# Cutting 1056 token columns into 512, 512 and 32 in place of three times 352 in the dense projections of a hybrid decoder step

## The reference, cut to what matters

```python
def mlp(x, w_up, w_down):
    h = jax.nn.relu(x @ w_up)          # 1024 -> 4096
    return (h * h) @ w_down            # 4096 -> 1024

p  = rmsnorm(x, norm_mix) @ w_in_rec                  # 1024 -> 3080, then conv, RG-LRU, gated delta
x += concat(rg_y, dn_y) @ w_out_rec                   # 1024 -> 1024
x += mlp(rmsnorm(x, norm_mlp[0]), w_up[0], w_down[0])
p  = rmsnorm(x, norm_mix[1]) @ w_in_att               # 1024 -> 2120, then index scores, top-k, softmax
x += o @ w_out_att                                    # 1024 -> 1024
x += mlp(rmsnorm(x, norm_mlp[1]), w_up[1], w_down[1])
```

## Time and profile before

| | |
|---|---|
| runs | 3677.41, 3677.54, 3678.38 us (median 3677.54) |
| span of the profiled execution, first to last instruction | 3673.0 us |
| own time of the profiled execution | not given apart from the three runs, which stand 4.4 to 5.4 us above the span |
| busy, share of the span | PE 83%, PEld 75%, DVE 37%, ACT 20%, POOL 25% |
| mean granted TensorE clock | 0.889 of full speed |
| DMA | 152.44 MB, 42 GB/s |

### The profile page before, as it was taken

The page is one execution under the profiler, slowest core; times in us unless marked ns, Lnnn a source line. Parts: engine busy times, 40 slices in busy tenths (PEclk is TensorE's granted clock), DMA queues, the critical chain, the costliest instruction groups (busy, mean ns, idle before and its releaser), DMA issues.

```text
span 3673.0 us, 44605 instructions
## 1 busy us (share of the span) xinstructions
PE 3060.5 (83%) x17464; PEld 2770.9 (75%) x17464; DVE 1360.5 (37%) x1847; ACT 741.1 (20%) x1136; POOL 933.8 (25%) x588
## 2 busy tenths in 40 slices
PE   6999276667799999999999860278888999999996
PEld 5998156666689999999999320134578899999996
DVE  6631644443542222222511177775203422222225
ACT  3321411112110000000200256424311200000001
POOL 2432022220233333333433010000002233333331
PEclk8999678887799999999999575589868999999998
DMA  4111000001211111111211110000122111111111
GB/s 132 46 46 29 17 1 0 0 0 49 76 35 46 46 43 46 46 46 46 90 46 33 50 38 20 0 22 2 55 72 76 32 46 43 46 46 43 46 46 61
DMA packets 237187, 152.44 MB, mean 42 GB/s; under 512 B 21243, under 2 KB 232884, under 8 KB 236169
## 3 DMA queue, kind: packets, MB, share of 16 engines
q1 hardware_dynamic: 226000, 121.17, 11.5%
q10 hardware_dynamic: 11116, 30.33, 2.3%
HBM read 133.46 MB, written 18.01 MB: 41 GB/s over the span
## 4 chain that ended last, share of the span: by engine, by line
PE 69%; DVE 11%; ACT 5%; issue 2%; DMA 0%; DVEq 0%; ACTq 0%; POOL 0%; POOLq 0%
PE ps L1298 50%; ACT junk L815 2%; PE ps L1389 2%; PE ps L1396 2%; PE ps L644 2%; PE ps L713 2%; PE ps L677 1%; PE ps L1347 1%; DVE sc L944 1%; PE ps L1401 1%; DVE hl L2028 1%; ACT dn_yy L1658 1%; PE ps L615 1%; PE ps L746 1%; PE ps L601 1%
## 5 line engine op out<-in xcount | busy, mean ns | idle before, releaser
L1189 POOL TENSOR_TENSOR w_hi<-w_raw,ones 128x512 fp32r<-128x512 f32 (+1 forms) x250 | 370.9, 1484 | 2216.3 <-PE ps L1298 1973.2
L1298 PE MATMUL ps<-xh,w_hi 128*128 128x352 f32 x2928 | 638.4, 326 | 59.3 <-DVE xl L1979 20.7
L1298 PE MATMUL ps<-xh,w_lo 128*128 128x352 f32 x2928 | 634.5, 324 | 0.0
L1298 PE MATMUL ps<-xl,w_hi 128*128 128x352 f32 x2928 | 633.8, 325 | 0.0
L1298 PEld LDWEIGHTS ps<-xh,w_hi 128*128 128x128 f32 x2928 | 502.6, 190 | 63.7 <-issue 59.9
L1298 PEld LDWEIGHTS ps<-xh,w_lo 128*128 128x128 f32 x2928 | 505.8, 189 | 0.0
L1298 PEld LDWEIGHTS ps<-xl,w_hi 128*128 128x128 f32 x2928 | 500.5, 189 | 0.0
L1192 POOL TENSOR_TENSOR w_lo<-w_raw,w_hi 128x512 fp32r<-128x512 f32 (+1 forms) x250 | 480.5, 1922 | 19.6
L2044 DVE TENSOR_TENSOR x<-x,ps 128x1056 f32<-128x1056 f32 x128 | 160.5, 1254 | 501.8 <-PE ps L1298 501.8
L1298 PE MATMUL ps<-hh,w_hi 128*128 128x352 f32 x1536 | 333.0, 325 | 13.7 <-DVE hl L2028 13.7
L1298 PE MATMUL ps<-hh,w_lo 128*128 128x352 f32 x1536 | 331.1, 323 | 0.0
(11 more groups left out here) (363 smaller groups left out, 3100.9 us busy)
## 6 DMA issues: line engine op xcount, KB each, us to landing
w_raw<-in_w_up SPq DMA_DIRECT2D x64, 512.0 KB, 4.1
w_raw<-in_w_down SPq DMA_DIRECT2D x128, 256.0 KB, 2.8
w_raw<-in_w_in_rec SPq DMA_DIRECT2D x24, 512.0 KB, 3.9
x_spill<-x ACTq DMA_DIRECT2D x2, 4224.0 KB, 13.2
x<-x_spill ACTq DMA_DIRECT2D x4, 2112.0 KB, 8.3
w_raw<-in_w_in_att SPq DMA_DIRECT2D x16, 512.0 KB, 3.8
kpg<-in_cache_k SPq DMA_DIRECT2D x64, 128.0 KB, 2.0
vpg<-in_cache_v SPq DMA_DIRECT2D x64, 128.0 KB, 2.0
```

The source lines that it names most:

```text
L1189: pool.tensor_tensor(w_hi[:, j % 2, 0:n], w_raw[:, j % 2, 0:n], ones[:, 0:1].to_broadcast([P, n]), ALU.mult).then_inc(w_hi_done, 1)
L1298: mm = pe.matmul(ps[:, 3 * (j % 2) + t, 0:n], w[:, j % 2, k * P:(k + 1) * P], r[:, k, c0:c0 + n], start=(k == 0 and p == 0), stop=(k == kt ...
```

## The change

All seven uses of `unit` in the dense projections pass `CUTS512` in place of `CUTS352`. The view of a set of banks becomes one run of 1056 columns, since 512, 512 and 32 columns fill three banks without a hole, and every eviction reads that run. In the convolution units two DVE instructions for the prompt columns become one, and the count of the chain in that loop goes from 8 to 6 a turn. The sums of squares keep `CUTS352`.

```diff
-        def set_view(j, c0, n):
-            return ps[:, 3 * (j % 2) + c0:3 * (j % 2) + c0 + n, :]
+        def set_view(j):
+            return flat(ps[:, 3 * (j % 2):3 * (j % 2) + 3, :])[:, 0:TOK]
...
-            units(pe, FIRST["att_in"] + 1, 16, 2, unit(KT, xh, xl, CUTS352))
+            units(pe, FIRST["att_in"] + 1, 16, 2, unit(KT, xh, xl, CUTS512))
...
-                dve.tensor_tensor(oq[:, ds(j + off - first, 1), :].rearrange("p o (a t) -> p (o a) t", a=3),
-                                  set_view(j, 0, 3)[:, :, 0:352], r3, ALU.mult).then_inc(set_free, 1)
+                dve.tensor_tensor(flat(oq[:, ds(j + off - first, 1), :]), set_view(j), rstd[:, :], ALU.mult).then_inc(set_free, 1)
...
-                unit(KT, xh, xl, CUTS352, ready)(j, 0)
+                unit(KT, xh, xl, CUTS512, ready)(j, 0)
...
-                        unit(KT, xh, xl, CUTS352)(first + q, c * 12)
+                        unit(KT, xh, xl, CUTS512)(first + q, c * 12)
...
-                        unit(FT, hh, hl, CUTS352, None if q else hidden)(first + FT + q, c * 12)
+                        unit(FT, hh, hl, CUTS512, None if q else hidden)(first + FT + q, c * 12)
...
-                own.did(dve.tensor_tensor(ub[:, 3:3 + 704].rearrange("p (a t) -> p a t", a=2), set_view(j, 0, 2)[:, :, 0:352],
-                                          r3[:, 0:2, :], ALU.mult))
-                own.did(dve.tensor_tensor(ub[:, 3 + 704:3 + SEQ], ps[:, 3 * (j % 2) + 2, 0:SEQ - 704], rstd[:, 704:SEQ], ALU.mult))
+                own.did(dve.tensor_tensor(ub[:, 3:3 + SEQ], set_view(j)[:, 0:SEQ], rstd[:, 0:SEQ], ALU.mult))
...
-            with own.loop(8, 8) as i:
+            with own.loop(8, 6) as i:
...
-                            dve.scalar_tensor_tensor(hu[:, q % 2, :].rearrange("p (a t) -> p a t", a=3),
-                                                     set_view(first + q, 0, 3)[:, :, 0:352], 0.0, r3, ALU.max, ALU.mult)\
+                            dve.scalar_tensor_tensor(hu[:, q % 2, :], set_view(first + q), 0.0, rstd[:, :], ALU.max, ALU.mult)\
...
-                xm = x[:, m, :].rearrange("p (a t) -> p a t", a=3)
-                dve.tensor_tensor(xm, xm, set_view(j, 0, 3)[:, :, 0:352], ALU.add).then_inc(set_free, 1)
+                dve.tensor_tensor(x[:, m, :], x[:, m, :], set_view(j), ALU.add).then_inc(set_free, 1)
```

More of the change, by code:

```diff
@@ L756, in rest_of_pe @@
             pe.wait_ge(S["mix_l"], 2 * KT)
-            units(pe, FIRST["att_out"], U_ATT_OUT, 2, unit(KT, xh, xl, CUTS352))
+            units(pe, FIRST["att_out"], U_ATT_OUT, 2, unit(KT, xh, xl, CUTS512))
             mlp(1)
@@ L898, in rest_of_dve @@
             norm_mean(2, 3 - 3 * (first % 2))
-            r3 = rstd[:, :].rearrange("p (a t) -> p a t", a=3)
             def project_unit(j, off):
                 dve.wait_ge(mm_out, j + off + 3)
-                dve.tensor_tensor(oq[:, ds(j + off - first, 1), :].rearrange("p o (a t) -> p (o a) t", a=3),
-                                  set_view(j, 0, 3)[:, :, 0:352], r3, ALU.mult).then_inc(set_free, 1)
+                dve.tensor_tensor(flat(oq[:, ds(j + off - first, 1), :]), set_view(j), rstd[:, :], ALU.mult).then_inc(set_free, 1)
             units(dve, first, 16, 2, project_unit)
@@ L909, in rest_of_dve @@
             for out in (ki[0:IDX_D, :], ki[IDX_D:2 * IDX_D, :]):
[L910 to L913, removed]
+                own.did(dve.tensor_tensor(out, set_view(j)[0:IDX_D], rstd[0:IDX_D, :], ALU.mult))
+            dve.tensor_tensor(wi[:, :], set_view(j)[IDX_D:IDX_D + IDX_H], rstd[IDX_D:IDX_D + IDX_H, :], ALU.mult).then_inc(set_free, 1)
             mlp_start(dve, "dve")
@@ L1304, in _ @@
             first_unit(0, FIRST["rec_in"])
-            units(pe, FIRST["rec_in"] + 1, 24, 2, unit(KT, xh, xl, CUTS352))
+            units(pe, FIRST["rec_in"] + 1, 24, 2, unit(KT, xh, xl, CUTS512))
             end_phase(pe, "pe")
@@ L1463, in _ @@
             pe.wait_ge(S["mix_l"], KT)
-            units(pe, FIRST["rec_out"], U_REC_OUT, 2, unit(KT, xh, xl, CUTS352))
+            units(pe, FIRST["rec_out"], U_REC_OUT, 2, unit(KT, xh, xl, CUTS512))
             def mlp(l):
@@ L1783, in conv_unit @@
                 dve.wait_ge(S["conv_done"], u + 1)
-                own.did(dve.tensor_tensor(ub[:, 3:3 + 704].rearrange("p (a t) -> p a t", a=2), set_view(j, 0, 2)[:, :, 0:352],
-                                          r3[:, 0:2, :], ALU.mult))
-                own.did(dve.tensor_tensor(ub[:, 3 + 704:3 + SEQ], ps[:, 3 * (j % 2) + 2, 0:SEQ - 704], rstd[:, 704:SEQ], ALU.mult))
+                own.did(dve.tensor_tensor(ub[:, 3:3 + SEQ], set_view(j)[:, 0:SEQ], rstd[:, 0:SEQ], ALU.mult))
                 heads = ub[:, 3 + SEQ:UB].rearrange("p (b t) -> p b t", b=DEC_BATCH)
                 dve.tensor_tensor(heads[:, :, 3:],
-                                  ps[:, 3 * (j % 2) + 2, SEQ - 704:352].rearrange("p (b t) -> p b t", b=DEC_BATCH),
+                                  set_view(j)[:, SEQ:].rearrange("p (b t) -> p b t", b=DEC_BATCH),
                                   rs_s, ALU.mult).then_inc(set_free, 1)
@@ L1807, in body @@
                     dve.wait_ge(mm_out, u + 3)
-                    dve.tensor_tensor(dst[:, ds(u - first, 1), :].rearrange("p o (a t) -> p (o a) t", a=3),
-                                      set_view(j, 0, 3)[:, :, 0:352], r3, ALU.mult).then_inc(set_free, 1)
+                    dve.tensor_tensor(flat(dst[:, ds(u - first, 1), :]), set_view(j), rstd[:, :], ALU.mult).then_inc(set_free, 1)
                 return body
@@ L1815, in _ @@
             dve.wait_ge(mm_out, j + 3)
-            dve.tensor_tensor(rows_raw[:, :].rearrange("p (a t) -> p a t", a=3), set_view(j, 0, 3)[0:64, :, 0:352],
-                              r3[0:64], ALU.mult).then_inc(set_free, 1)
+            dve.tensor_tensor(rows_raw[:, :], set_view(j)[0:64], rstd[0:64, :], ALU.mult).then_inc(set_free, 1)
             dve.wait_ge(set_free, 2 + U_REC_IN)
@@ L1984, in body @@
                     dve.wait_ge(mm_out, j + off + 3)
-                    xm = x[:, ds(j + off - first, 1), :].rearrange("p o (a t) -> p (o a) t", a=3)
-                    dve.tensor_tensor(xm, xm, set_view(j, 0, 3)[:, :, 0:352], ALU.add).then_inc(set_free, 1)
+                    xm = flat(x[:, ds(j + off - first, 1), :])
+                    dve.tensor_tensor(xm, xm, set_view(j), ALU.add).then_inc(set_free, 1)
                     add_square(n, j + off - first, (j - first) % 2)
```

## The result

Four runs of the changed kernel took 4067.73 to 4072.62 us, median 4071.41, against 3677.47 (3675.20 to 3678.38) before: a ratio of 1.1069 with a 95% interval of 1.1056 to 1.1083. It is slower by 394 us, where 359 were forecast (4036 in a range of 3900 to 4110).

What follows compares the result with a forecast made beforehand. PE's pace in the dense projections' matmuls was taken as the bound. The cut's +367 us (0.0823 us a triple, 4464 triples) less 8 in chunk waits gave +359 on 3673.0; with the median's 4.5 offset 4036 us, range 3900 to 4110.

Steps and rivals of the forecast that it cites:

- The bound: Dense projections' matmul line, half of the span: in these 2220 us the time is PE's pace, nearly one for one.
- The short piece costs a load, 0.11 us: Each triple's 32-column piece costs a weight load, 0.11 us (bounds 0.105 to 0.125), not its columns.
- The faster rival: Loads run two matmuls ahead, so the short piece costs only its 32 columns: −192 us, 3490 us; chance 0.05.
- The 512-column piece costs 0.2294: Each long piece of a triple: 0.215 us of columns plus 0.0144 extra; bounds 0.215 to 0.236.
- float32r's extra once a matmul: The 0.0144 us a 352-column matmul takes beyond bf16's column pace, charged once a matmul whatever its length; chance 0.58.
- The rival by the column: The extra grows with columns: 0.236 us a long piece, 0.582 a triple, 4095 us; chance 0.17.
- The chunk waits, −8 us: PE's stand of 0.86 us inside each MLP chunk, 16 times, waiting for DVE, shrinks to 0.4: −8 us in all.
- Cold starts and first units, zero: First input-projection unit grows 2 us at no cost; about 25 triples at stage starts, at double time, add 2: zero together.
- Evictions, zero: Reading one run of 1056 columns gains 0 to 10 ns an eviction, under 1 us in all: 0.
- the instruction saved in the convolution: One DVE instruction less in 16 convolution units, 0.12 us each, hidden behind a busy PE: 0.
- No drop of the clock: Against the rival that the clock drops as PE streams less of the time; chance 0.05 together with two loads.
- the double: At the lower level, 1.2 GHz, columns and load take twice as long and the loss doubles: +2 us at stage starts.

Runs made afterwards that it cites:

- run 2: The changed kernel with pieces of 128, 512 and 416 columns in place of 512, 512 and 32: 3886.83 us, ratio 1.0573 to the kernel before.
- run 3: The kernel before, three pieces of 352, with one more 32-column matmul a triple into a bank that nothing reads: 4178.92 us, ratio 1.1364.
- run 5: The changed kernel with the 32-column piece in the first of three passes only: 3749.69 us, ratio 1.0192 to the kernel before.
- run 4: The kernel before with one more 32-column matmul a triple, which uses only 64 of the 128 weight columns: 4164.85 us, ratio 1.1324.
- Run 1: The changed kernel with pieces of 256, 512 and 288 columns, the first at the end of its bank: 3665.75 us, 0.9967 of before.
- run 8: The changed kernel with pieces of 288, 512 and 256 columns, starting at columns 0, 288 and 800: 3670.54 us, 0.9986 of before.

## Why the prediction was right

- *The bound.* Right: the stretches of L1294 took the whole loss, and no other engine did more work.
- *The short piece costs a load, 0.11 us.* Right in its size and, as far as the runs go, in its reason: 32, 128 and an added 32 columns all cost 0.11 (runs 2, 3, 5), and it isn't the short matmul's own load (run 4). The faster rival, loads two matmuls ahead, is out: it needed less than 0.0277 us.
- *The 512-column piece costs 0.2294.* This is the term that was mis-sized. From the triple it is (0.5763 − 0.109) / 2 = 0.2337 us, from run 5 0.233. The step that failed was to charge float32r's extra once a matmul. Run 1 separates the two readings: 256 and 288 columns took 0.1185 + 0.1334 = 0.2519 us, where an extra by the column gives 0.2507 and one a matmul 0.2572. The rival by the column (0.236, with 4095 us) was the better reading, a little too dear at 512. The error stays small because the whole extra is only 0.0144 us a matmul. A triple lost 0.0898 us in place of 0.0823, times 4464 that is +401 in place of +367, and this is the difference to the forecast.
- *The chunk waits, −8 us.* The stand went to 0.31 us, 16 × 0.55 = −9. Right.
- *Cold starts and first units, zero.* The sum over the nine stages rose by 404, three more than the triples account for; the first unit's 2 us were hidden as said (PE idles 9.83 us in place of 11.59 behind it, until DVE's sum of squares is there). At the lower level the loss of a triple does double: 0.88 us before and 1.07 after, against 0.4865 and 0.5763 (rows in the last section). Right within what can be read.
- *Evictions, zero.* Right: 1254 ns in both forms, and the instruction saved in the convolution made no difference.
- *No drop of the clock.* Right by stage, 0.97 to 1.00. But the first 9 us of the input projection ran at a granted clock of 0.81, where the kernel before had 1.00 (lines below the list). PE had idled 1.63 us just ahead of it, and 1.64 before; what made the clock fall in one and not in the other is open. Four triples between 68.06 and 71.93 us take 0.85 to 1.07 us there in place of 0.58, some 1.6 us in all, which is about half of the three above.

The stretch with the clock, first of the kernel before and then of the changed one:

```profile
66.00:75.00 9.00, 9.00 (x56) 9.00 (x57) 1.00 0.01 2
...
66.90:76.00 9.10, 9.09 (x40) 7.64 (x40) 0.81 0.01 2
```

The sum closes: +401 − 9 and a few us of starts make the 397.5 by which the span grew.

## What to carry to other kernels

Where each matmul loads its own weights, a piece is free only while its stream is longer than the next load, here 0.109 us. That is about 235 float32r columns, an estimate from 0.1622 us for 352; the runs show that 128 columns are too few and 256 are enough. Cut a length that isn't a multiple of 512 into pieces that all stay above this, and not into full banks and a rest. Pieces of 256, 512 and 288 columns, the first at the end of its bank, keep the result contiguous without the loss. Read the pace from many matmuls in a row and the floor from the step between the first two loads after a wait.

## What was not expected of the hardware

float32r streams more slowly than bf16: 0.46 ns a column at 352 columns and 0.456 at 512, against 0.42 for bf16 (two steps), at the same granted clock of 1.00. The price of a cut also depends, by some 1 ns a matmul, on where its pieces start or on their order (0.4851 and 0.4834 us a triple in runs 8 and 1, which have the same three lengths; three of 352 take 0.4865).

At the lower level, 1.2 GHz, a float32r triple of 352 does not take twice as long. In the timelines of PE, before and after, at a granted clock of 0.50:

```profile
36.25 1.08 PE L1298 MATMUL ps<-xh,w_lo 128*128 128x352 f32 x3
37.13 1.08 PE L1298 MATMUL ps<-xh,w_hi 128*128 128x352 f32 x3
...
69.97 1.23 PE L1294 MATMUL ps<-xl,w_hi 128*128 128x512 f32 x3
71.04 1.04 PE L1294 MATMUL ps<-xh,w_lo 128*128 128x512 f32 x3
```

From start to start it is 0.88 us, 1.81 times the 0.4865 us at full clock, or 0.83 ns a column. The prediction took the double. Twice bf16's 0.42 would be 0.84, so what float32r takes beyond bf16 at full clock is not seen here; no bf16 matmul at the lower level was compared.
